# Identity first, rows spread by three matmuls, and the sample values and decay rows ahead of a 2 MB unit, in one step of a hybrid decoder

## What is computed

```python
hn = rmsnorm(h, norm_mix)
u = hn @ w_in
xa_c = silu(causal_conv(xa))
q, k = xc @ w_q, (xc @ w_k) * DH_A ** -0.5
v = xa_h @ w_v
C1 = dec * C0 + einsum('bhsd,bhse->bhde', kw, v)
h = q C-read, normalised
xbc_c = silu(causal_conv(xbc)); y = ssd(xbc_c, dt, S0)
h = h + concat(h_a, y) @ w_out
h = h + hier_moe(rmsnorm(h, norm_ffn))
y = rmsnorm(h, norm_final)
```

## Time and profile before

| | |
|---|---|
| three runs, median | 786.35 us |
| the profiled execution, its own time | 785.29 us |
| its span on the core | 783.4 us |
| TensorE (PE) busy | 746.2 us, 95% of the span |
| VectorE (DVE), ScalarE (ACT), Pool busy | 272.7, 215.1, 30.1 us |
| the chain that ended last | PE 73%, DMA 17%, DVE 5%, ACT 4% |
| moved by DMA | 263.71 MB, 337 GB/s over the span, 425 to 429 from the nineteenth of 40 slices on |
| mean granted TensorE clock | 0.99 |

### The profile page before, as it was taken

The page is one execution under the profiler, slowest core; times in us unless marked ns, Lnnn a source line. Parts: engine busy times, 40 slices in busy tenths (PEclk is TensorE's granted clock), DMA queues, the critical chain, the costliest instruction groups (busy, mean ns, idle before and its releaser), DMA issues.

```text
span 783.4 us, 10029 instructions
## 1 busy us (share of the span) xinstructions
PE 746.2 (95%) x4013; PEld 420.6 (54%) x4013; DVE 272.7 (35%) x649; ACT 215.1 (27%) x622; POOL 30.1 (4%) x89
## 2 busy tenths in 40 slices
PE   6998999998999999999999999999999989989995
PEld 5886888876788888633434335334343333333232
DVE  4944656768977301430031031300310210311204
ACT  4227666739765001600100001001001001001003
POOL 6100000010000100000000000000000000000000
PEclk9999999999999999999999999999999999999998
DMA  9954467956895586779999999999999999999992
GB/s 255 314 202 129 154 191 242 344 190 189 272 311 190 233 359 284 309 283 428 427 428 427 425 428 427 427 427 425 428 426 427 428 425 425 426 429 427 427 394 80
DMA packets 76349, 263.71 MB, mean 337 GB/s; under 512 B 7382, under 2 KB 46554, under 8 KB 62840
## 3 DMA queue, kind: packets, MB, share of 16 engines
q1 hardware_dynamic: 74512, 259.02, 84.7%
q0 software_dynamic: 1568, 3.91, 1.4%
q10 hardware_dynamic: 216, 0.07, 0.0%
HBM read 251.15 MB, written 11.99 MB: 336 GB/s over the span
## 4 chain that ended last, share of the span: by engine, by line
PE 73%; DMA 17%; DVE 5%; ACT 4%; issue 1%; POOL 1%; SPq 0%; POOLq 0%; DVEq 0%; ACTq 0%
PE bank L2304 22%; PE bank L1888 10%; PE bank L2384 8%; PE bank L2161 7%; DMA ring<-in_w_up 5%; DMA arena<-in_w_down 5%; DMA xn<-in_w_up 5%; PE bank L2271 4%; PE bank L1876 4%; PE bank L2329 2%; PE bank L1975 2%; ACT h_tok L1002 1%; PE bank L2282 1%; DVE h_tok L1430 1%; PE bank L1835 1%; PE bank L2317 1%
## 5 line engine op out<-in xcount | busy, mean ns | idle before, releaser
L2304 PE MATMUL bank<-ring,arena 128*64 128x512 f32 x640 | 144.4, 596 | 5.7 <-DMA ring<-in_w_up 5.6
L1888 PE MATMUL bank<-arena,ring 128*128 128x264 f32 (+1 forms) x448 | 107.7, 395 | 4.6 <-DVE arena L1578 1.8
L1888 PEld LDWEIGHTS bank<-arena,ring 128*128 128x128 f32 x448 | 83.6, 191 | 20.6 <-issue 3.0
L2304 PEld LDWEIGHTS bank<-ring,arena 128*64 128x64 f32 x640 | 43.6, 137 | 93.5 <-issue 80.8
L509 DVE COPY arena<-bank 64x512 f32<-64x512 f32 x15 | 10.2, 683 | 214.6 <-PE bank L2384 214.6
L2384 PE MATMUL bank<-ring,arena 128*64 128x512 f32 x272 | 60.6, 593 | 1.3 <-DMA ring<-in_w_down 1.3
L1755 DVE TENSOR_TENSOR arena<-bank,WG 128x512 f32<-128x512 f32 x16 | 16.9, 1056 | 122.1 <-PE bank L2304 122.1
L2304 PE MATMUL bank<-arena 128*64 128x512 f32 x240 | 54.8, 597 | 3.8 <-DMA arena<-in_w_up 2.5
L2161 PE MATMUL bank<-arena,ring 128*128 128x264 f32 x256 | 58.4, 387 | 0.0
L2161 PEld LDWEIGHTS bank<-arena,ring 128*128 128x128 f32 x256 | 48.3, 190 | 8.5 <-issue 0.3
L1227 ACT ACTIVATE arena<-bank 128x512 f32<-128x512 f32 x15 | 9.0, 597 | 145.9 <-PE bank L2317 145.9
(11 more groups left out here) (397 smaller groups left out, 850.8 us busy)
## 6 DMA issues: line engine op xcount, KB each, us to landing
ring<-in_w_gate SPq DMA_DIRECT2D x20, 2048.0 KB, 29.2
ring<-in_w_up SPq DMA_DIRECT2D x20, 2048.0 KB, 34.1
ring<-in_w_down SPq DMA_DIRECT2D x17, 2048.0 KB, 31.4
ring<-in_w_in SPq DMA_DIRECT2D x9, 2048.0 KB, 10.4
arena<-in_w_down SPq DMA_DIRECT2D x7, 2048.0 KB, 33.3
arena<-in_w_up SPq DMA_DIRECT2D x6, 2048.0 KB, 24.8
arena<-in_w_gate SPq DMA_DIRECT2D x6, 2048.0 KB, 36.6
out<-h_tok SPq DMA_DIRECT2D x16, 512.0 KB, 4.2
```

Source lines behind the costliest of these rows:

```text
L1888: last = mm(b[:, q0:T], slot_k(UNIT_SLOT[u], 512)[:, k, o:o + P], hT[:, k, q0:T], start=(k == 0), stop=(k == KD - 1))
L2304: last = mm(b[CAP * half:CAP * (half + 1), :], XG[:, k, (e % 2) * CAP:(e % 2 + 1) * CAP], w(kk)[:, half * 512:(half + 1) * 512], start=(k ...
```

## The change

- Opening: Pool makes the identity first and signals it by itself. TensorE issues `turning` (transposes of the identity into a bank that nothing reads) 14, 8, 6 and 4 times between its pieces. The last 24 rows are normalised by ScalarE; the raw samples are turned alone, last. The Sqrt table is loaded ahead of ScalarE's small loads, the Exp table later.
- Rows: VectorE multiplies `RS` and `RX` into block-diagonal operands `RSD`, `RXD`; three matmuls with ones spread them. These and the 15 transposes (`rows_turned`) go ahead of the eighth xa tile.
- Sample values: a signal and a copy of their own, ahead of ScalarE's `head_in(0)`.
- SP: the unit U_B + 1 (2 MB) goes behind the decay rows and the first value rows.
- ScalarE: `row_exps` and two tanh one tile earlier; head 0's `evac` ahead of `decay_state(1)`.
- Pool: eight small loads (router weights and biases, gain, two conv copies) go behind head 0's output.
- Tail: the two `norm_final` matmuls go ahead of the last expert's up projection, into other banks.

```diff
-            mixer_unit(U_B + 1)
...
             sp.wait_ge(s.rows_out, 48)
             v_rows(0)
+            mixer_unit(U_B + 1)
             for h in range(HA):
...
             link(g.memset(epst[:, 1:2], 1.0))
+            link(g.memset(ident[:], 0.0))
+            g.affine_select(out=ident[:], in_=ident[:], compare_op=ALU.not_equal, fill=1.0, base=0,
+                            pattern=[[-1, P]], channel_multiplier=1).then_inc(s.consts, 1)
             g.memset(ones[:], 1.0)
-            g.memset(ident[:], 0.0)
...
                 head_state_out(pool, h)
+                if h == 0:
+                    pool.dma_start(wr[:, :, 0:4], w_r1[0].rearrange("(k p) g -> p k g", p=P)).then_inc(s.prev_in, 16)
...
             act.wait_ge(s.pv_ready, 1)
+            m = NB + META
+            a.activation(xn[0:m, 2, :], h_tok[0:m, 2, :], ACT.Copy, scale=st3[0:m, 6:7]).then_inc(s.xn_ready, 1)
+            act.wait_ge(s.pv_ready, 2)
...
-                if n == 6:
+                if n == 5:
                     row_exps()
-            tanh_of_conv(0)
-            tanh_of_conv(1)
+                    tanh_of_conv(0)
+                    tanh_of_conv(1)
             for q in range(2):
                 lct_copy(q, bank[6 + q], s.lct_sb)
+            sample_values()
             act.wait_ge(s.tm_ready, 1)
-            sample_values()
             head_in(0)
...
             conv_taps(0)
             conv_taps(1)
+            dve.wait_ge(s.rows_exp, 1)
+            v.tensor_tensor(RSD.rearrange("p (h x) -> p h x", x=16), RS[:, :].unsqueeze(1).to_broadcast([HA, HA, 16]),
+                            bc_last(ident[0:HA, 0:HA], 16), ALU.mult)
+            for j in range(2):
+                last = v.tensor_tensor(RXD[j].rearrange("p (c x) -> p c x", x=17), RX[:, :].unsqueeze(1).to_broadcast([HB, KD, 17]),
+                                       bc_last(ident[0:HB, j:HB:2], 17), ALU.mult)
+            last.then_inc(s.rows_exp, 1)
...
+            def turning(n, b):
+
+                for _ in range(n):
+                    tr(bank[b][:, 0:P], ident[:, :], ident[:, :])
+
+            turning(14, 7)
             for i in range(2):
                 pe.wait_ge(x_in[i], 16)
...
+                if i == 0:
+                    turning(8, 7)
             pe.wait_ge(s.xn_ready, 1)
...
+            turning(6, 7)
+            pe.wait_ge(s.xn_ready, 2)
             pe.wait_ge(s.params_in, 16 * 8)
...
+                mm(bank[5][:, 0:HA * 16], ones[0:HA, :], RSD, start=True, stop=True)
+                for j in range(2):
+                    mm(bank[5][j * HD:(j + 1) * HD, P:P + KD * 17], ones[0:HB, 0:HD], RXD[j], start=True, stop=True)
...
                 last.then_inc(s.u_ps, 1)
+                if n0_ == 6:
+                    rows_turned()
...
+                if h == 0:
+                    pe.wait_ge(s.vs_sb, 2)
                 for j, t0 in enumerate(S_TILES):
                     last = mm(bank[2][:, j * P:(j + 1) * P], XC[:, h, t0:t0 + P], wk[:, h, :], start=True, stop=True)
...
                     if x_ == NX - 2:
+                        pe.wait_ge(s.x_again, 16 * 2)
+                        for c in range(2):
+                            mm(bank[c][:, :], ones[FROW:FROW + 1, :], NFROW[:, c * 512:(c + 1) * 512], start=True, stop=True)\
+                                .then_inc(s.gbc_ps, 1)
                         project(x_ + 1, 1, 0)
```

## The result

The changed kernel takes **774.75 us** (median of four runs, 774.53 to 775.05) against 786.07 of the kernel before: ratio 0.9845, 95% interval 0.9813 to 0.9877, 11.3 us. The forecast was 778.0 with a range from 775.4 to 781.6: the direction was right, the size was not, by 3.25 us. The profiled execution took 774.53 us (span 772.8), where the sum had 776.9. The median stands 0.22 us over it; for the kernel before the forecast had 1.06.

A forecast was written before the change was run, and what follows sets the result against it. The mixer's end was taken to start the expert stream. Terms -0.3 + 2.1 + 1.7 - 0.2 + 1.3 + 0.2 + 1.7 + 1.9 = 8.4 us gave median 778.0 us, range 775.4 to 781.6.

The forecast's parts named there:

- What bounds it: Whole kernel: the expert weight stream starts when the mixer is done, so time gained early is carried to the end.
- Opening: Up to the gate matmuls: earlier start but 32 dummy transposes ahead of the parameters; 0.3 us lost, ends 1.6 gained, 3.3 lost.
- The rival in which the dummies stay slow: Opening: transposes never reach the full clock, 3.0 us more, 781.0 us in all; chance 0.05.
- Rows by three matmuls: Ahead of the eighth xa tile: three matmuls replace 24 little ones, 2.1 us gained.
- The clock behind it: Behind the eight xa tiles: shorter run of tiny operations keeps TensorE's upper clock, 1.7 us gained, ends 0 and 1.7.
- Values and decay rows: Head 0: earlier copy and rows ahead of the 2 MB remove waits, 1.3 us at scores, 0.2 at state reads.
- Evacuation: Second xbc tile: ScalarE empties xbc tile 0 ahead of its eight state activations, 1.7 us of wait gained.
- Nothing behind the head loop: From the head loop's end to the tail: no gain or loss of its own was forecast, 0 us.
- Pool: Pool's eight small loads, moved behind head 0's output, arrive before VectorE needs them: free.
- The slower rival: Router weights: Pool's loads come one by one, VectorE stands 18 us, 796 us in all; chance 0.04.
- Tail: Last expert: norm_final broadcasts moved ahead of the last up projection, 1.9 us gained, ends 1.0 and 2.0.
- From the profiled execution to the median: Whole kernel: profiled execution forecast at 776.9 us, median 1.06 us above it, as in the kernel before.

The follow-up runs named there:

- the three traces of before: The unchanged kernel before, traced once for the prediction and twice more beside the experiments; spans 782.4, 784.4 and 784.1 us.
- the changed kernel's second trace: The changed kernel run again with no edit, on another occasion; span 776.0 us, median 776.81 us, ratio 0.9855 to the kernel before.
- the second trace of before: The kernel before run again with no edit, the first of two such repeats; span 784.4 us.

## Why the prediction was wrong

- **What bounds it: right.** A later start of the second xbc tile is carried on: delays of 1.6 to 8 us in the opening were the same at the head loop's end, and SyncE's longest wait is unchanged.
- **Opening: the reason was wrong.** -0.3 us was forecast, and 0.39, -0.06 and -0.05 came against the three traces of before, within the opening's scatter; 13.97 us, from which the sum started, is the latest of the three. The parameters start at 10.04 us where the sum had 10.8. The dummies do not stand in anyone's way: without them the gates start 0.17 us later, not earlier. They are worth 1.7 us behind that point, where the clock otherwise falls in the gates; the sum had no such term. (The kernel before, without dummies, had no fall there: 4.00 us for the gates.) The rival in which the dummies stay slow (3.0 us more) did not come: after 22 dummies and transposes at 0.23 to 0.24 us each, and eight in 1.20, eight took 1.04 us.
- **Rows by three matmuls: right**, 0.70 us against 0.7. **The clock behind it: right in size (1.58 of 1.7 us), wrong in its ground.** The words "with a full tile of 3.78 us behind them" were half of the argument; with 24 ahead of that tile the clock falls within the tile. It was the shorter run of little operations, not the place, and the new place cost 0.48 us where 0.2 was forecast.
- **Values and decay rows: right that the trip is hidden, too small at the reads.** The trip was just hidden, with 0.66 us to spare. The 0.2 us ahead of the reads came from the one trace with a wait of 0.18; the stage gave 0.46, 1.30 and 0.85 against the three. The two parts were not independent: the unit's new place was given no price of its own; undone alone it costs 7.92 us at the second xbc tile, most of it through a wait of 5.24 us and the low clock behind it.
- **Evacuation: right** for the wait (1.61 to 1.89 against 1.7).
- **Here the failed step lies:** "From that tile on (73.23 us) TensorE has no idle time until the head loop's end, so the time at which it starts is what I work out". That priced the 1.72 us ahead of the second xbc tile as idle time alone and put all behind it at 0; of the clock only the fall at 54 us was in the sum. But the clock falls while TensorE is busy, too. In two of three traces of the kernel before a fall stands in that tile, the 1.80 us of the stage table; the trace that the prediction read had none there. No trace of the changed kernel or its variants has one in that tile, but for the one with a wait of 5.24 us ahead. That removing the wait removed the fall is not shown: put back alone, a wait of 1.44 us brought none. What the runs do show is fewer falls over all. The mean granted clock is 0.9895 over the 43 runs of the kernel before that stand beside the experiments and 0.9940 over eight of the changed kernel; by span times 1 less clock (an estimate) 8.2 and 4.6 us of clock are missing, a step of 3.6 us where the forecast had 1.7. Which part of the change took the rest stays open.
- **Nothing behind the head loop: wrong in the profiled pair, chance.** 0.95 us there is one fall that before's first trace had at 328 us and the changed kernel's first had not; it was there (at 321 us) in the changed kernel's second trace and in neither of before's new ones.
- **Pool: right**, 0.02 us. The slower rival fell: a stall of 2.88 us, the last issue at 76.22 us, the product at 92.79 without a wait.
- **Tail: right**, 1.74 to 1.78 against 1.9.
- **From the profiled execution to the median:** the forecast added 1.06 us, by which before's median stood over its profiled execution, the fastest of its four. For the changed kernel it is 0.22. So 0.84 of the 3.25 us is scatter of the kernel before and says nothing of the change.

Against the second trace of before, the terms that were forecast make 9.6 us in place of 8.4, the stage with the fall 1.8 and the other two 0.1: 11.5, at a span that is 784.4 - 772.8 = 11.6 longer. The range failed because it was made of bounds on these terms, and no case in it let the clock give back more than the one fall at 54 us.

## What to carry to other kernels

Price a stretch of TensorE by its waits and by the clock behind them, and the clock as a chance: in two of three traces of the kernel before a fall stood behind a wait of 1.73 us, and a wait of 1.44 us put back brought none. 24 little matmuls in place of three cost 2.13 us themselves and 1.58 in what came next. One trace does not show which falls a kernel usually has; take two or three of the kernel before ahead of summing. Where a wait can't go, dummy transposes in it kept the clock up, though that saved less than the falls. And an early copy can be worth nothing while a large load still stands ahead of it on the queue.

## What the runs showed of the hardware

- A whole fall takes 1.7 us of clock in the windows above, 4.00 x (1 - 0.57) or 5.00 x (1 - 0.66). In time it cost 1.80 us in the second xbc tile, 0.95 us behind the router and next to nothing at 181 us, where a later wait took it up. Falls came behind waits of 0.90 to 5.24 us or runs of little operations, in one execution and not in the next with the same instructions at the same times (one and three falls in two traces of the changed kernel). The Trainium skill (TensorE: Matmul & The Clock Gate, Part 1: The HAM clock gate) has activity judged on a clock of its own that does not start with the kernel; falls that come and go at the same place agree.
- The granted clock in the profile reads 1.00 from the start, while the first 22 transposes take 0.23 to 0.24 us each and the eight at 7.64 us 0.13.
- 32 KB written behind a 2 MB load on the same queue took 7.5 us, ahead of it 1.97.
